# Sliding-window attention: the normalising diagonals made by GpSimd, and the halves of the output weights made during the linear attention

## The reference, cut to what matters

```python
scores = jnp.einsum('bnqhgd,bnkhd->bnhgqk', qb, kb).astype(jnp.float32) * (ATT_HEAD_DIM ** -0.5)
...
probs = jax.nn.softmax(jnp.concatenate([scores, sink], axis=-1), axis=-1)[..., :-1]
out = jnp.einsum('bnhgqk,bnkhd->bnqhgd', probs.astype(v.dtype), vb)
...
b = jnp.cumsum(gt, axis=2)
inter = jnp.einsum('bhtd,bhde->bhte', qt * jnp.exp(b), state)
...
mixed = jnp.concatenate([att, go], axis=-1) @ w_out[l]
x = x + gate1 * mixed
```

## Time and profile before

| what | value |
|---|---|
| median of three runs | 2973.14 us |
| the profiled execution, its own time | 2973.76 us |
| its span (first to last instruction) | 2972.0 us |
| PE, DVE, ACT, POOL busy | 2735.0, 1661.8, 937.6, 1350.8 us |
| mean granted clock of TensorE | 0.966 of full |

### The profile page before, as it was taken

How to read it: one execution, slowest core, us unless ns; L and a number is a source line. 1 busy time by engine, 2 the same in 40 slices (tenths; PEclk the granted TensorE clock), 3 DMA queues, 4 the chain that set the end, 5 groups by cost and what they waited for, 6 DMA issues and landing times.

```text
span 2972.0 us, 32441 instructions
## 1 busy us (share of the span) xinstructions
PE 2735.0 (92%) x12074; PEld 2069.3 (70%) x12074; DVE 1661.8 (56%) x3130; ACT 937.6 (32%) x1682; POOL 1350.8 (45%) x995
## 2 busy tenths in 40 slices
PE   7989999899998999999896789999999999989944
PEld 6856888777888678888775668888888754434411
DVE  1032145575144354420306639999996999856686
ACT  3275334665243332222336223111112940000001
POOL 3433543665455134444333226444445954444465
PEclk9999999999999999999998889999999999999977
DMA  4311233332243146653220037999999369999998
GB/s 158 103 53 36 85 100 87 120 106 74 97 139 124 49 133 201 198 163 100 80 85 29 22 107 254 376 389 392 376 390 407 104 246 381 391 411 409 409 382 296
DMA packets 221245, 599.11 MB, mean 202 GB/s; under 512 B 24465, under 2 KB 49314, under 8 KB 220578
## 3 DMA queue, kind: packets, MB, share of 16 engines
q1 hardware_dynamic: 137312, 301.22, 29.7%
q0 software_dynamic: 75968, 275.81, 24.5%
q10 hardware_dynamic: 7810, 20.02, 2.0%
HBM read 585.36 MB, written 7.41 MB: 199 GB/s over the span
## 4 chain that ended last, share of the span: by engine, by line
PE 70%; DVE 12%; DMA 10%; issue 3%; POOL 3%; ACT 3%; SPq 0%; DVEq 0%; ACTq 0%; POOLq 0%
PE ps L1796 15%; PE ps L1293 13%; PE ps L1295 13%; PE ps L1294 13%; DMA rows<-in_v,expert 5%; DMA rows<-in_u,expert 5%; DVE ps L2497 3%; PE ps L1259 1%; POOL wlo L1095 1%; PE ps L1391 1%; PE ps L1824 1%; POOL rows L1204 1%; DVE rows L2483 1%; PE ps L1813 1%; PE ps L1478 1%
## 5 line engine op out<-in xcount | busy, mean ns | idle before, releaser
L1095 POOL TENSOR_TENSOR wlo<-wraw,whi 128x1024 fp32r<-128x1024 f32 x258 | 627.5, 2444 | 869.2 <-ACT whi L581 868.8
L581 ACT ACTIVATE whi<-wraw 128x1024 fp32r<-128x1024 f32 x258 | 269.2, 1058 | 708.8 <-PE ps L1295 594.6
L1293 PE MATMUL ps<-hhi,whi 128*128 128x512 f32 x1096 | 432.9, 395 | 19.4 <-DVE hlo L1948 5.3
L1836 PE MATMUL ps<-stream,hg 128*128 128x512 f32 x1024 | 442.5, 595 | 8.2 <-DMA stream<-in_v 8.2
L1796 PE MATMUL ps<-haff,stream 128*128 128x256 f32 x2048 | 444.1, 380 | 2.2 <-ACT stg L999 2.2
L1295 PE MATMUL ps<-hhi,wlo 128*128 128x512 f32 x1096 | 429.9, 392 | 0.0
L1294 PE MATMUL ps<-hlo,whi 128*128 128x512 f32 x1096 | 429.8, 392 | 0.0
L1796 PEld LDWEIGHTS ps<-haff,stream 128*128 128x128 f32 x2048 | 390.1, 191 | 55.7 <-ACT stg L999 2.4
L1204 POOL DMA_INDIRECT rows<-in_u,expert x256 | 264.7, 1034 | 267.5 <-DVE hid L2483 141.2
L1836 PEld LDWEIGHTS ps<-stream,hg 128*128 128x128 f32 x1024 | 195.3, 191 | 255.3 <-issue 245.5
L1204 POOL DMA_INDIRECT rows<-in_v,expert x256 | 248.1, 969 | 260.5 <-DVE ps L2497 123.2
(11 more groups left out here) (465 smaller groups left out, 4376.4 us busy)
## 6 DMA issues: line engine op xcount, KB each, us to landing
stream<-in_ut SPq DMA_DIRECT2D x128, 512.0 KB
stream<-in_v SPq DMA_DIRECT2D x128, 512.0 KB
wraw<-in_w_in SPq DMA_DIRECT2D x96, 512.0 KB
wraw<-in_w_ada SPq DMA_DIRECT2D x48, 512.0 KB
wraw<-in_w_gu SPq DMA_DIRECT2D x88, 256.0 KB
wraw<-in_w_down SPq DMA_DIRECT2D x22, 512.0 KB
decs<-acs_kept ACTq DMA_DIRECT2D x16, 512.0 KB, 3.7
wraw<-in_w_br_ssm SPq DMA_DIRECT2D x16, 512.0 KB
```

The lines of the kernel that those rows point to most:

```text
L581: act.activation(whi[:, n % WSLOTS, 0:kn, :], wraw[:, n % WSLOTS, 0:kn, :], ACT.Copy).then_inc(w_hi, 1)
L1095: pool.tensor_tensor(wlo[:, n % WSLOTS, 0:kn, :], wraw[:, n % WSLOTS, 0:kn, :], whi[:, n % WSLOTS, 0:kn, :].bitcast(F32), ALU.subtract).th ...
L1293: pe.matmul(dst, lh, rh, start=k == 0, stop=False)
L1836: ins = pe.matmul(ps[:, 2 * i + half, :], hg[:, n, P * i:P * i + P], stream[j][:, 4 * half:4 * half + 4, :], start=n == 0, stop=n == NKEYS ...
```

## The change

- The diagonals go from ACT to POOL: in place of eight scaled copies per block, two products of the identity, repeated for four heads, with `srec`, repeated along the row. Each raises `sw_p` by four.
- DVE waits, before it overwrites `srec` in blocks 1 to 3, for the diagonals of the block before.
- On ACT, `group(G["in4"])` rounds nothing; the four chunks of `out0` are rounded one each behind levels 2, 3, 4 and 5.
- On POOL, the four small halves of `out0` move behind the last level's `gl_q`; ahead of `q_in` stand the diagonals of blocks 0 and 1, between `q_in` and `k_out` those of block 2, and behind `k_out` those of block 3, ahead of the first `gl_q`.

```diff
--- before.py
+++ after.py
@@ -580,8 +580,9 @@
                         used(act, slot_before(n))
                     act.activation(whi[:, n % WSLOTS, 0:kn, :], wraw[:, n % WSLOTS, 0:kn, :], ACT.Copy).then_inc(w_hi, 1)
 
-            def group(g, jobs, evac):
-                round_upto(ahead(GROUPS[g][2]))
+            def group(g, jobs, evac, rounds=True):
+                if rounds:
+                    round_upto(ahead(GROUPS[g][2]))
                 for j in jobs:
                     acc_wait(act, g, j)
                     ins = evac(j, 4 * (g % 2) + j)
@@ -924,18 +925,10 @@
                     act.activation(sw[:, h, lo:], sw[:, h, lo:], ACT.Exp, bias=st[:, 8 + h:9 + h], accum_out=st[:, 16 + h:17 + h])
                 act.activation(st[:, 24:32], st[:, 24:32], ACT.Exp).then_inc(s("sw_exp"), 1)
 
-            def sw_diagonals(b):
-                act.wait_ge(s("sw_rec"), b + 1)
-                if b:
-                    act.wait_ge(s("sw_tr"), 4 * b)
-                for h in range(SW_HEADS):
-                    act.activation(sw_dg[:, h, :], ident, ACT.Copy, scale=srec[:, h:h + 1]).then_inc(s("sw_p"), 1)
-
             sw_exp(0)
             for b in range(NT):
-                sw_diagonals(b)
                 if b == 0:
-                    group(G["in4"], (0, 1), to_tokens(gv_s, 0))
+                    group(G["in4"], (0, 1), to_tokens(gv_s, 0), rounds=False)
                 if b:
                     act.wait_ge(s("sw_o"), b)
                 for n in (0, 2):
@@ -953,6 +946,7 @@
                 act.activation(k_tok[:, c, :], ps[:, 4 + c, 0:256], ACT.Copy).then_inc(s("ktok_ready"), 1)
             for lv in range(2, LEVELS):
                 level_decay(lv)
+                round_upto(GROUPS[G["in4"]][2] + min(lv - 1, WSLOTS))
             act.preload_act_table_set("sqrt_and_others")
             for c in range(NT + 1):
                 if c < NT:
@@ -1168,17 +1162,30 @@
             after("xo1")
             after("gu10")
             after("dn1")
-            after("in4")
-
+            rest_upto(GROUPS[G["in4"]][2])
+
+            def sw_diagonals(b):
+                pool.wait_ge(s("sw_rec"), b + 1)
+                if b:
+                    pool.wait_ge(s("sw_tr"), 4 * b)
+                for h in range(0, SW_HEADS, 4):
+                    pool.tensor_tensor(sw_dg[:, h:h + 4, :], ident.unsqueeze(1).to_broadcast([P, 4, P]),
+                                       srec[:, h:h + 4].unsqueeze(2).to_broadcast([P, 4, P]), ALU.mult).then_inc(s("sw_p"), 4)
+
+            sw_diagonals(0)
+            sw_diagonals(1)
             pool.wait_ge(s("gla_act"), 2)
             pool.tensor_tensor(q_in[:], q_in[:], gq_t[:], ALU.mult).then_inc(s("qin_ready"), 1)
+            sw_diagonals(2)
             pool.wait_ge(s("gla_act"), 4)
             pool.tensor_tensor(k_out[:], k_out[:], gk_t[:], ALU.mult).then_inc(s("kout_ready"), 1)
+            sw_diagonals(3)
             for lv in range(LEVELS):
                 pool.wait_ge(s("gdec_ready"), lv + 1)
                 if lv >= 2:
                     pool.wait_ge(s("att_ready"), 4 * (lv - 1))
                 pool.tensor_tensor(gl_qs[lv % 2][:], gl_ds[lv % 2][:], gq_t[:], ALU.mult).then_inc(s("glq_ready"), 1)
+            after("in4")
             after("out1")
             after("pq1")
 
@@ -2302,6 +2309,8 @@
                 st = sw_stats[b % 2]
                 v.wait_ge(s("sw_exp"), b + 1)
                 link(v.tensor_tensor(sden, st[:, 16:24], st[:, 24:32], ALU.add))
+                if b:
+                    v.wait_ge(s("sw_p"), SW_HEADS * b)
                 v.reciprocal(srec, sden).then_inc(s("sw_rec"), 1)
                 if b:
                     sw_low(b - 1)
```

## The result

The changed kernel takes 2958.12 us (median of five runs, 2955.63 to 2960.58); beside it the kernel before took 2972.52 (five runs, 2971.05 to 2974.84). The ratio is 0.995, with a 95% interval of 0.9936 to 0.9965. That is 14.4 us less (by the interval 10.4 to 19.0), where 11.0 were forecast, and the time lies inside the range.

What follows compares the result with a forecast made beforehand. PE held 70% of the chain, so edits of ScalarE and GpSimd pay only where PE or DVE waits for them. Terms -6.6 - 2.4 - 1.4 + 0.2 - 0.8 = -11.0 us gave 2962.1 us, range 2956.5 to 2969.5.

Steps and rivals of the forecast that it cites:

- Halves away from block 0: VectorE's log decays and scans run shorter without GpSimd's small halves beside them: -6.6 us, between nothing and 7.2.
- Block 0: Sliding attention: PE starts block 0's transposes up to 0.5 us later, taken as a loss of 0.2 us.
- Diagonals on GpSimd: Sliding attention: products at 1.2 us each; PE's starts gain 2.4 us in block 2 and 1.4 in block 3.
- TensorE's clock: Block 3's transposes in the sliding attention get shorter as PE's waits shrink: -0.8 us, between nothing and 2.7.
- Rounding behind the levels: ScalarE's roundings of 0.97 us each hide in its waits ahead of levels: cost nothing, 4 us if uncovered.
- the halves behind the last level: GpSimd's four halves end at 1667.9, ten us ahead of the output projection, and do not hold masked copies: nothing.
- VectorE slow by itself: Rival, 10%: log decays stay long without GpSimd beside them, so the 6.6 us are not there; 2969.5 us.
- GpSimd's product dear: Rival, 7%: a diagonals' product takes 4.8 us, deciding from about 3.2; slower kernel, +12.5, 2985.6 us.
- Clock takes some back: Rival, 10%: one more 1.2 GHz stretch in the levels or output projection costs 3.3 us; 2965.4 us.
- Clock stays up: Rival, 15%: TensorE keeps 2.4 GHz, block 3 is 2.7 us shorter, block 2 at most 1.4 more; 2958.8 us.
- Won and lost elsewhere: Rival, 5%: the expert stage's transfers eat most of the gain, or the moved halves are late; about 2971 us.
- The rule that would put the products on VectorE: Skill's rule against two-input work on GpSimd; products on VectorE were forecast at some 2 us less gain.

Runs made afterwards that it cites:

- two kernels with fillers on GpSimd: The change plus unused GpSimd work behind block 0's diagonals: four products that read (2957.93 us) or eight fills that only write (2954.92 us).
- fillers on TensorE: Unused TensorE products behind blocks 0 to 2: six added to the change (2954.38 us), or two added to decays early (2949.77 us).
- diagonals alone: The kernel before with only the diagonals' products moved to GpSimd, rounding and small halves where they were: 2959.66 us, ratio 0.9959.
- halves alone: The kernel before with roundings behind the levels and small halves behind the last one, diagonals still on ScalarE: 2963.2 us, ratio 0.9968.
- decays early: The change with VectorE's block 0 reciprocals ahead of its `gv_s` copies, and log decays and scans ahead of block 1's maxima: 2953.78 us, ratio 0.9946.
- the kernel that rounds early: The change, but ScalarE rounds the four chunks in one piece ahead of `gv_s`, as before: 2957.87 us, ratio 0.9955.
- reading filler: The change plus four unused GpSimd products of 128x1024 that read constants, behind block 0's diagonals: 2957.93 us, ratio 0.9961.

## Why the prediction was right, point by point

The gain is some 3 us larger than forecast, 2958.12 us lies just below the bounds of the forecast itself (2959 to 2965), and the 11.0 lies inside the interval of the measurement. So the size of the whole tests the parts little; the profiles do.

**Halves away from block 0: forecast -6.6, measured -7.5 on VectorE's run.** Mechanism as forecast: 12.06 to 4.61 us. Line 2278 was priced like an operation with two inputs (1.22) and took 0.69; the scans were priced at 3.1 and took 2.63 together, since back to back each costs less than its own 0.40. As the end was bounded at 7.2, the term went 0.3 past its bound. The second part, that ScalarE would be ahead of VectorE in block 1, held too: the last exponential's sum ended at 1578.99, VectorE's run at 1580.48.

**Block 0: forecast +0.2, measured +0.7.** The diagonals of four heads come together, and PE began 0.5 us later behind the reciprocals; its transposes took 0.25 longer. From the reciprocals of block 0 to those of block 1, the first two terms together: 16.95 to 10.20, -6.75 against -6.4.

**Diagonals on GpSimd: priced at 1.2 us a product, measured 1.04,** the least and the greatest 2 ns apart. Block 2's start came -2.4 in the forecast: between the reciprocals of blocks 2 and 3 it is 13.41 to 10.58, -2.8. The ground given for counting it, that block 3's exponentials wait for the third step of the transposes, no longer held: they now began behind VectorE's maxima, so an even earlier third step would have given nothing more. Block 3's start: 3.01 to 1.91, -1.1 against -1.4; here a step was missing. The start was not set by the product but by line 2303, behind value products that waited for VectorE's copy and then ran mostly at 1.2 GHz (a grant of 0.53). In the two kernels with fillers on GpSimd, where the same value products took 1.99 us, block 3 started 1.52 us after its reciprocals, -1.5.

**TensorE's clock: forecast -0.8, measured -2.3 in block 3. This is the term that was mis-sized.** I had set it between nothing and 2.7 and taken 0.8 because the clock had been at 1.2 GHz after a wait of 1.91 us too. But block 3's transposes now ran wholly at 2.4 GHz (6.08 to 3.81). That is all there was: with 0.61 of the clock granted before, the 2.7 was out of reach. In the sliding attention the forecast missed 2.2 us, and this term is 1.5 of them.

The rest of what the profiled executions show beyond the forecast lies in the query stage, 3.2 us. The forecast had one rival in which the clock gave something and one in which it took something back later; neither had a later stage that gains. In the profiles of all kernels run here this stage takes either about 146.6 or about 149.8 us (148.1 and 148.7 with fillers on TensorE): 146.6 in the change, twice, and in five edits of it, 149.8 in the kernel before, diagonals alone, halves alone and decays early. It was edited in none of them, and what decides it, no run here tells. Nor is it shown that the 3.2 us belong to the change and not to the one execution that was profiled. The medians of diagonals alone and halves alone lie 3.2 and 6.8 us above the change's of the same group; their sliding stretches alone make 2.6 and 5.8 of that, and with the longer query stage it would be 5.9 and 9.1. Their profiled executions, which have the longer stage, were the slowest of each kernel, 4.2 and 3.3 us above its median.

**What cost nothing, as forecast.** Rounding behind the levels (shown by the kernel that rounds early); the halves behind the last level (they ended at 1655.08, the masked copies kept their 0.72 us, and levels with projection took 87.90 against 87.83); `q_in`, `k_out` and `gl_q` behind the products (the transposes of `k_out` waited 1.46 us, for the last `hhi`, before and after; the first two `gl_q` ended at 1609.51 and TensorE came to the levels at 1613.54).

**The rivals.** VectorE slow by itself: fell, by halves alone and the two fillers. GpSimd's product dear: fell, 1.04 against the 3.2 from which it would have decided. Clock takes some back: fell for the sum, since a stage got faster. Clock stays up, with 15% and 2958.8 us: its condition came true, in blocks 2 and 3 (3.81 us each), its sizes did not. In the sliding attention the clock gave 2.3 in block 3, where the rival had 2.7; block 2 came 0.4 beyond the forecast, where it had 1.4, because block 3's exponentials then waited for VectorE's maxima. That the measured time lies within 0.7 us of this rival's is in part luck. My ground against it, a low grant after a wait of only 1.91 us, was true and proved nothing about the other waits. Won and lost elsewhere: fell, the expert stage took 1109.51 us before and 1109.31 after. (The low end of the stated range, 2956.5, should have been 2956.8 by its own working.) The rule that would put the products on VectorE: fell, by 3.2 us in the stretch. The Trainium skill (GPSIMD Engine Reference, Engine selection) has GpSimd about twice as slow for two inputs; these products took 1.04 us there and 0.65 on VectorE, a factor of 1.6. What decided here was which engine PE waits for, and that is VectorE.

**What the sum hid.** Its parts were not the parts of the change. I gave 6.6 to the moved halves and 3.6 to the moved diagonals; alone, they give 7.2 and 10.4 in the stretch, and 13.2 together. The step left out is that ScalarE's rounding stood behind its own diagonals, so that the place of the diagonals also set when GpSimd's halves ran. The total was right since both were done.

## What to carry to other kernels

When VectorE's operations are two to six times as long as the same form elsewhere, look for what GpSimd reads at that time, and move that, before making VectorE's work smaller. The engine that does an operation fastest is not always the one to give it to; ask first whose other work is waited for: the two products of a block took 2.04 us on GpSimd and 1.29 on VectorE, and the kernel with the faster ones had a sliding stretch 3.2 us longer. And to see what a part of a change is worth, run it alone: an engine's list couples its parts.

## What the runs showed of the hardware, beyond what was expected

Very small operations of VectorE can be held as long as large ones (diagonals alone): two on eight elements took 2.31 and 1.50 us in place of 0.17 and 0.15 beside GpSimd's halves of about 2.4 us each, and ended with such a half; another, in the gap between two halves, took 0.15. A fill of 128x1024 on GpSimd took 1.05 us (8.44 / 8), a product of the same size 2.25 in the reading filler and 2.36 elsewhere; the fill held VectorE's one-input operation (1.29 in place of 0.69) and not those with two.

TensorE's clock was worth 1.6 to 2.3 us in one block: 32 transposes took 3.81 us at full grant, most often 5.44 where it was low, and 6.08 in block 3 of the kernel before. The length of the last wait alone doesn't say which: behind 1.89 us (the change, block 2) and 2.80 us (decays early, block 1) they took 3.81, behind 2.90 and 2.32 us (the same kernel, blocks 2 and 3) 5.44. Behind the same wait of 2.19 us, block 2's value products took 3.51 us in the change and 1.99 with a filler on GpSimd. Two unused products in such a wait, 1.13 us in all, kept the clock in block 3 and not in block 2, and, counting all later stages, came with 4.0 us less time (2953.78 to 2949.77). How the clock will lie a hundred microseconds and more behind the edit stayed open.
